# One transformer layer on one core: the first pair's operands used in place, the load of W_down moved, and three reorderings

## The reference

```
h      = rmsnorm(x) * (1 + scale1) + shift1
q,k,v,p = h @ w_in                       # 512 | 128 | 128 | 512 columns
merged = [rmsnorm(attention(q, k, v)), rmsnorm(causal_pool(p))]
x      = x + gate1 * (merged @ w_out)
h2     = rmsnorm(x) * (1 + scale2) + shift2
out    = x + gate2 * ((silu(h2 @ w_gate) * (h2 @ w_up)) @ w_down)   # 2816 wide
```

## Time and profile before

| | us |
|---|---|
| median of 3 runs (lowest, highest) | 1058.69 (1054.54, 1060.44) |
| the profiled execution | 1058.78 |
| its span, first to last instruction | 1057.0 |
| TensorE busy in it | 985.1 (93%) |
| VectorE busy | 701.2 (66%) |
| mean granted TensorE clock | 0.982 |

### The profile page before, as it was taken

One profiled execution on the slowest core, in us unless ns is written; L12 is line 12 of the kernel. 1 busy time (PEld: TensorE's weight loads), 2 busy tenths in 40 slices (PEclk: granted clock), 3 DMA queues, 4 the chain that ended last, 5 costly groups with the idle time before them and its releaser, 6 DMA issues.

```text
span 1057.0 us, 13418 instructions
## 1 busy us (share of the span) xinstructions
PE 985.1 (93%) x4656; PEld 822.1 (78%) x4656; DVE 701.2 (66%) x1089; ACT 379.3 (36%) x722; POOL 211.7 (20%) x167
## 2 busy tenths in 40 slices
PE   6979999989979849999999999999999999999998
PEld 6768888888867637878878787887878788787876
DVE  4658888784777857566566756656675666666554
ACT  2646667575333523123130412313041231304120
POOL 2033333334211005021110302111030211103010
PEclk9989999999999979999999999999999999999999
DMA  9935443255134196433344543334454343445223
GB/s 365 360 131 219 140 140 140 100 160 198 42 120 140 60 297 240 159 120 131 128 180 159 198 159 119 133 126 178 159 198 159 119 142 126 169 159 198 80 80 159
DMA packets 82725, 168.79 MB, mean 160 GB/s; under 512 B 5392, under 2 KB 50176, under 8 KB 82688
## 3 DMA queue, kind: packets, MB, share of 16 engines
q1 hardware_dynamic: 77456, 157.37, 41.9%
...
## 4 chain that ended last, share of the span: by engine, by line
PE 70%; DMA 10%; DVE 10%; ACT 3%; SPq 2%; issue 2%; POOL 1%; ACTq 0%; DVEq 0%
PE ps L1553 22%; PE ps L1555 21%; PE ps L1554 21%; DMA bs<-bs_scratch 7%; DMA wi_raw<-in_w_in 2%; PE ps L1664 1%; SPq L408 1%; DVE x L1179 1%; PE ps L1766 1%; SPq L410 1%; DMA bs_scratch<-stg 1%; DVE xn L1335 1%; DVE ring L1369 1%; DMA sinks<-in_attn_sinks 1%; DVE nmax L1248 1%
## 5 line engine op out<-in xcount | busy, mean ns | idle before, releaser
L1413 DVE TENSOR_TENSOR x<-x,ps 128x512 f32<-128x512 f32 x176 | 120.7, 686 | 83.6 <-PE ps L1555 82.8
L1025 POOL TENSOR_TENSOR wd_lo<-raw_d,wd_hi 128x1024 fp32r<-128x1024 f32 x22 | 57.4, 2627 | 425.7 <-ACT wd_hi L796 425.7
L1553 PE MATMUL ps<-h_hi,ring 128*128 128x512 f32 x352 | 138.1, 392 | 1.2 <-DVE h_lo L1362 0.9
L1554 PE MATMUL ps<-h_lo,ring 128*128 128x512 f32 x352 | 137.4, 390 | 0.0
L1555 PE MATMUL ps<-h_hi,ring 128*128 128x512 f32 x352 | 137.4, 390 | 0.0
L1553 PE MATMUL ps<-wd_hi,act_hi 128*128 128x512 f32 x352 | 136.9, 389 | 0.0
L1554 PE MATMUL ps<-wd_lo,act_hi 128*128 128x512 f32 x352 | 136.9, 389 | 0.0
L1555 PE MATMUL ps<-wd_hi,act_lo 128*128 128x512 f32 x352 | 136.9, 389 | 0.0
L1553 PE MATMUL ps<-bs,ring 128*128 128x512 f32 x264 | 106.0, 401 | 28.7 <-DMA bs<-bs_scratch 27.8
L1554 PE MATMUL ps<-bs,ring 128*128 128x512 f32 x264 | 104.5, 396 | 0.0
L1555 PE MATMUL ps<-bs,ring 128*128 128x512 f32 x264 | 104.2, 395 | 0.0
...
## 6 DMA issues: line engine op xcount, KB each, us to landing
...
raw_g<-in_w_gate SPq DMA_DIRECT2D x11, 1024.0 KB, 5.0
raw_u<-in_w_up SPq DMA_DIRECT2D x11, 1024.0 KB, 6.9
raw_d<-in_w_down SPq DMA_DIRECT2D x11, 1024.0 KB, 7.9
...
```

What stands on the lines that cost most here:

```text
L1025: pool.tensor_tensor(wd_lo[:, q, :], raw_d[:, q, :], wd_hi[:, q, :].bitcast(F32), ALU.subtract).then_inc(wd_lo_done, 1)
L1413: dve.tensor_tensor(xt, xt, bank(DB[j % 4]), ALU.add).then_inc(down_evac, 1)
L1553: pe.matmul(dst, s_hi, m_hi, start=start, stop=False, skip_group_check=onto)
L1554: pe.matmul(dst, s_hi, m_lo, start=False, stop=False, skip_group_check=onto)
```

## The change

1. `bs2`, two buffers of 8 KB per partition, takes T4. In the first pair T3 and T4 of tiles 6 and 7 are split straight into `bs` and `bs2`, at the columns where `S3` and `A22` read them. T3 and T4 of tiles 2 and 4 still go through the stage to DRAM and come back by three DMAs (`t_back`) after the last out-projection chain, whose buffers `bs` and `bs2` overlap. B22 goes through the stage for all four tiles. T3 and T4 of tiles 6 and 7 are also stored to DRAM, for the later pairs (`store_direct`).
2. In the order of tiles 2 and 4, B22 is split last.
3. `load_down` of pair p is issued behind the first stream of pair p; it was issued behind the last stream of pair p-1. That of pair 0 comes after the first pair's `A22`.
4. `m_low` of tiles 3 to 7 goes from GpSimd to VectorE, behind `mixed_sum(t, 1)`.
5. `bias_tiles` (VectorE) and the product on `wpl` (GpSimd) go behind the first tile's work of iteration 0; folds and scalings are spread anew.
6. ScalarE and VectorE: the rows of h2 ahead of the square; the first weight parts and sums ahead of `mixed_sum(6, 1)`; the fourth token sum a function of its own; tile 6's T3 ahead of `norm_x1(7)`.

```diff
+        bs2 = [place(f"bs2_{h}", [P, KT // 2, HALF], BASE + (104 + 16 * h) * KB, F32R) for h in range(2)]
...
-        FOLDS = (3, 5, 5, 5, 5, 1, 0, 0)
-        SCALED = ((), (), (), (), (), (0, 1, 2), (3, 4, 5), (6, 7))
+        FOLDS = (4, 4, 4, 4, 4, 4, 0, 0)
+        SCALED = ((), (), (), (), (), (), (0, 1, 2, 3, 4), (5, 6, 7))
...
-        T_ORDER = [(t, w) for t in (2, 4) for w in (T3, T4, B22, T2, T1)] + [
+        T_ORDER = [(t, w) for t in (2, 4) for w in (T3, T4, T2, T1, B22)] + [
...
-        STG_ORDER = [x for x in T_ORDER if x[1] in STREAMED]
+        STG_ORDER = [x for x in T_ORDER if x[1] == B22 or x[1] in STREAMED and x[0] < 6]
...
+            if (t, w) in STG_ORDER:
                 return stg[STG_ORDER.index((t, w)) % 2][:, low]
+            cols = slice(HALF1.index(t) * P, (HALF1.index(t) + 1) * P)
+            if w == T3:
+                return bs[:, :, low, cols]
+            if w == T4:
+                return bs2[low][:, :, cols]
...
-                    if not first and k < KT // 2 - 1:
-                        sp.wait_ge(bs_used, (KT // 2 - 1) * (3 * p + n - 1) + k + 1)
-                    elif not first:
+                    if k < KT // 2 - 1:
+                        sp.wait_ge(bs_used, (KT // 2 - 1) * (3 * p + n - 2) + k + 1)
+                    elif first:
+                        sp.wait_ge(prod_done, prod(0, S3, 1))
+                    else:
...
+            def store_direct(t, w):
+                sp.wait_ge(t_lo, T_ORDER.index((t, w)) + 1)
+                u = HALF1.index(t)
+                for h in range(2):
+                    sp.dma_start(bs_dram[STREAMED.index(w)][:, :, h, u * P:(u + 1) * P], t_dest(t, w, h).bitcast(F32)
+                                 ).then_inc(t_out, 16)
...
-            load_down(0, first=True)
-            store_stage(6, T3)
-            store_stage(7, T3)
-            store_stage(6, T4)
+            sp.wait_ge(stg_out[0], 32 * 3)
+            sp.wait_ge(stg_out[1], 32 * 3)
+            sp.dma_start(bs[:, :, :, 0:2 * P].bitcast(F32), bs_dram[0][:, :, :, 0:2 * P]).then_inc(t_back, 16)
+            for h in range(2):
+                sp.dma_start(bs2[h][:, :, 0:2 * P].bitcast(F32), bs_dram[1][:, :, h, 0:2 * P]).then_inc(t_back, 16)
+            store_direct(6, T3)
+            store_direct(7, T3)
+            store_direct(6, T4)
+            store_direct(7, T4)
+            load_raw(1, 0)
+            load_raw(1, 1)
+            store_stage(6, B22)
+            store_stage(7, B22)
+            sp.wait_ge(t_out, 32 * 4)
             sp.wait_ge(stg_out[0], 32 * 4)
             sp.wait_ge(stg_out[1], 32 * 4)
-            load_stream(0, 0, first=True)
-            store_stage(7, T4)
-            load_raw(1, 0)
-            load_raw(1, 1)
-            sp.wait_ge(stg_out[1], 32 * 5)
-            load_stream(0, 1)
-            store_stage(6, B22)
-            store_stage(7, B22)
-            sp.wait_ge(stg_out[0], 32 * 6)
-            sp.wait_ge(stg_out[1], 32 * 6)
-            load_stream(0, 2)
-            load_down(1)
+            load_stream(0, 2, first=True)
+            sp.wait_ge(prod_done, prod(0, A22, 1))
+            load_down(0, first=True)
             def pair_loads(p, last=False):
                 load_stream(p, 0)
+                load_down(p)
                 if not last:
                     load_raw(p + 1, 0)
                     load_raw(p + 1, 1)
                 load_stream(p, 1)
                 load_stream(p, 2)
-                if not last:
-                    load_down(p + 1)
...
+                if t - 1 in HALF1:
+                    h2_rows_act(t - 1)
                 square_x1(t)
                 if t - 1 in HALF0:
                     h2_high(t - 1)
-                if t - 1 in HALF1:
-                    h2_rows_act(t - 1)
...
-                if t == 6:
-                    act.wait_ge(g2_red_done, 1)
-                    a_high(0, A11, 0, 0, first=True)
-                    a_high(0, A11, 1, 0, first=True)
...
                     t_high(t - 1, T3)
                     t_high(t - 1, T4)
-                    t_high(t - 1, B22)
                     t_high(t - 1, T2)
                     t_high(t - 1, T1)
-            act.wait_ge(oa_chain, NT)
-            a_high(0, A12, 0, 0, first=True)
-            a_high(0, A12, 1, 0, first=True)
+                    t_high(t - 1, B22)
+                if t == 5:
+                    act.wait_ge(g2_red_done, 1)
+                    a_high(0, A11, 0, 0, first=True)
+                    a_high(0, A11, 1, 0, first=True)
+                    act.wait_ge(oa_chain, NT)
+                    a_high(0, A12, 0, 0, first=True)
+                    a_high(0, A12, 1, 0, first=True)
+            h2_rows_act(6)
             square_x1(7)
-            h2_rows_act(6)
+            act.wait_ge(t_back, 16 * 3)
+            t_high(6, T3)
             copy_p1(0, 0, first=True)
+            a_high(0, S2, 0, 0, first=True)
             norm_x1(7)
-            t_high(6, T3)
+            copy_p1(0, 1, first=True)
+            h2_rows_act(7)
             t_high(6, T2)
-            a_high(0, S2, 0, 0, first=True)
-            copy_p1(0, 1, first=True)
             a_high(0, S2, 1, 0, first=True)
-            h2_rows_act(7)
             t_high(7, T2)
             t_high(7, T3)
...
             act_high(silu_sb, 0, 0, 0, 1)
...
             second_half(0, 0)
+            down_high(0, first=True)
             with act.Fori(0, (NPAIR - 3) // 2) as j:
...
-
-            pool.wait_ge(const_in, 16 * 5)
-            pool.tensor_tensor(wpl[:, :, :], wpl[:, :, :], psc_bc, ALU.mult).then_inc(wpl_done, 1)
...
+                if it == 0:
+                    pool.wait_ge(const_in, 16 * 5)
+                    pool.tensor_tensor(wpl[:, :, :], wpl[:, :, :], psc_bc, ALU.mult).then_inc(wpl_done, 1)
...
-                if t + 3 < NT:
-                    m_low(t + 3)
...
-            bias_tiles()
...
+                if it == 0:
+                    bias_tiles()
...
-                dve.wait_ge(t_sum, n + 3)
+            def t_sum4(t):
+                xs = xn2[XBUF[PARTNER[t]]]
+                lo, up = slice(0, HALF), slice(HALF, D)
+                dve.wait_ge(t_sum, 4 * HALF1.index(t) + 3)
                 dve.tensor_tensor(xs[:, up], xs[:, up], xs[:, lo], ALU.subtract).then_inc(t_sum, 1)
...
             mixed_sum(0, 1)
             for t in range(1, NT):
                 if t + 1 < NT:
                     mixed_sum(t + 1, 0)
+                if t == NT - 2:
+                    a_low(0, A11, 0, 0)
+                    a_low(0, A11, 1, 0)
+                    dve.wait_ge(oa_chain, NT)
+                    a_low(0, A12, 0, 0)
+                    a_low(0, A12, 1, 0)
+                    a_sum13(0, 0, first=True)
+                    a_sum13(0, 1, first=True)
                 mixed_sum(t, 1)
+                if t + 2 < NT:
+                    m_low(t + 2)
                 if t < NT - 1:
                     h2_rows(t - 1)
+                    if t == NT - 2:
+                        a_sum2(0, 0, first=True)
                     if t - 1 in HALF0:
                         h2_low(t - 1)
                     else:
                         t_sums(t - 1)
+                        t_sum4(t - 1)
                         t_low(t - 1, T3)
                         t_low(t - 1, T4)
-                        t_low(t - 1, B22)
                         t_low(t - 1, T2)
                         t_low(t - 1, T1)
+                        t_low(t - 1, B22)
                     for k in FOLD2.get(t, ()):
                         fold_gate2(k)
-                if t == NT - 2:
-                    a_low(0, A11, 0, 0)
-                    a_low(0, A11, 1, 0)
-                    dve.wait_ge(oa_chain, NT)
-                    a_sum13(0, 0, first=True)
-                    a_sum13(0, 1, first=True)
-                    a_sum2(0, 0, first=True)
-                    a_sum2(0, 1, first=True)
-                    a_low(0, A12, 0, 0)
-                    a_low(0, A12, 1, 0)
+            a_sum2(0, 1, first=True)
             h2_rows(6)
             t_sums(6)
+            t_sum4(6)
             t_low(6, T3)
-            t_low(6, T2)
             a_low(0, S2, 0, 0)
-            a_low(0, S2, 1, 0)
             h2_rows(7)
             t_sums(7)
...
-            def stream_product(p, o, m, par, dst, start, n):
+            def stream_product(p, o, m, par, dst, start, n, direct=None):
                 pe.wait_ge(a_lo, prod(p, o, m))
-                if m == 0:
-                    pe.wait_ge(bs_in, 64 * (3 * p + n + 1))
+                if m == 0 and not direct:
+                    pe.wait_ge(bs_in, 64 * (3 * p + n - 1))
                 r = ring[m][(par + o) % 2]
                 for k in range(KT // 2):
-                    last = mm3(bank(dst[m]), r[:, 0, k, :], r[:, 1, k, :], bs[:, k, 0, :], bs[:, k, 1, :],
+                    b_hi, b_lo = (bs2[0][:, k, :], bs2[1][:, k, :]) if direct == T4 else (bs[:, k, 0, :], bs[:, k, 1, :])
```

(12 more changed lines are left out.)

17 lines of the change are left out of this document (12 added, 5 removed).

## The result

The changed kernel takes **1040.4 us** (median of 4 runs, 1040.1 to 1043.2) against 1059.0 us (4 runs of the kernel before beside it, 1054.5 to 1060.4). The ratio is 0.9837, its 95% interval 0.9803 to 0.9871: 1.3% to 2.0% faster. The span of the profiled execution went from 1057.0 to 1038.3 us. The forecast was 1040.4. The total is right; two of its terms are not, and they cancel.

What follows compares the result with a forecast made beforehand. TensorE was taken as the bound, busy 93% of the span, so only its waits and lower clock could yield time. Opening minus 4.8, x1 stage and first pair minus 13.6, W_down 0: 1058.8 - 18.4 = 1040.4 us, range 1033 to 1048.

Steps and rivals of the forecast that it cites:

- Opening, -4.8: Start of the kernel: TensorE's 5.7 us wait for `kn` goes, scores start at 67.6; minus 4.8 us, bounds 3 to 6.5.
- x1 stage: 260 to 350 us: five 1.7 us stalls, 4.9 us wait on `mixed_sum(6, 1)`, `A11` 3.2 us late; bounds minus 2 to plus 7.
- The price of the stretch: x1 stage: VectorE instructions meeting GpSimd's `m_low` ran longer (2.77 for 0.69 us); 2 us at five tiles.
- The sign that short waits leave the upper clock: x1 stage: after waits of 1.03 and 1.79 us the first product reads 0.47 and 0.50 us, taken as full clock.
- First pair: From 350 us: `S3` no longer waits for a stream, `S4` starts at 399 less 3.3 us.
- One sum without effect: First pair: W_down landed by 399, then scalings, copies and lows (5.2 + 2 + 5.2 us) end near 416, before `down(0)` at 425.
- W_down's load, 0 (bounds -2 to 0): Pair loop: issuing the load 11 us later changes nothing, since GpSimd's idle time covers it; 0 us, bounds minus 2 to 0.
- The argument from the last pair: Pair loop: the last pair loads no W_down yet waits 1.18 us, the same, so the load does not slow the stream.
- 1 (W_down held the stream up): Pair loop: W_down's load delayed the `S4` stream, so nine pairs' waits go (11.5 us): 1029 us; chance 0.12.
- 2: x1 stage and first pair: new waits eat most of the gain through lower clock and added work: 1051 us; chance 0.12.
- 3: First pair: the `S4` stream lands far too late, all lost after 411, 1063 us if at 415; chance 0.05.
- 4: First pair: it gives nothing because products wait for VectorE instead, only the opening is left: 1054 us; chance 0.05.

Runs made afterwards that it cites:

- e3: Kernel before, with only the bias tiles and GpSimd's product on `wpl` moved behind iteration 0's first work; 1053.3 us, ratio 0.9955.
- e9: Changed kernel with `m_low` of tiles 3 to 7 back on GpSimd, behind its rsqrt of the tile; 1038.9 us, ratio 0.9840.
- e2: Kernel before, with only W_down's load moved behind the first streamed load of its own pair; 1054.1 us, ratio 0.9965.
- e1: Changed kernel with W_down's load put back behind the third streamed load of the pair before; 1047.8 us, ratio 0.9904.
- e10: Kernel of e1, but from pair 1 on W_down's load brings 64 of 1024 columns (64 KB, not 1 MB); 1043.4 us, ratio 0.9879.
- e6: Changed kernel with pair 1's raw gate and up weights issued behind the stores of B22's last two tiles; 1044.8 us, ratio 0.9874.

## Why the prediction came out, step by step

- **Opening, -4.8**: right. -4.4 in the profiles, -4.8 alone (e3). The scores start at 66.99 us (67.6 forecast) behind 2.22 us of wait (3). The folds' new split cost nothing that shows: the out-projection starts at 254.88 us with it and at 255.30 in e3 without it.
- **x1 stage**: right in place and in size. Stalls of 1.64 us (1.7 forecast), four instead of five, the last one lying behind the products of `g2`. The wait on `mixed_sum(6, 1)` ended at 344.4 on the old clock (344.0) and was 4.66 us (4.9), with products of 0.63 us, the lower clock, until 344.2 (new clock) behind it. The price of the stretch, "2 us at five tiles", was right per meeting (2.1 us) and was met at four tiles in the kernel before (2.89, 6.19, 2.77 and 6.19 us for 0.75, 4.05, 0.69 and 4.05). What it was worth to TensorE was weighed too high: e9 brings all four back and is no slower. The sign that short waits leave the upper clock was read from the first product behind them (0.47 and 0.50 us), and that row cannot tell: behind 2.54 us of wait at 236.03 the kernel before reads 0.47 as well, and the granted clock in 236 to 246 us is 0.83. The conclusion was right by the clock itself, 1.00 in 295 to 300 and in 343 to 348 us.
- **First pair**: right in its chain, 3 to 4 us too optimistic. On the old clock: last transposes 363.3 (362.5), `S3` 377.8 (376.0), `S4` 399.8 (395.7). Three terms were too small. The three loads took 8.7 us from issue to ScalarE's start (347.41 to 356.12), not 7.5. The wait ahead of the transposes was 5.14 us, not about 4, and "the lower clock as before" lasted to 364.45, so `A12` ended 1.85 us late (372.35 for 370.5). And the stream: its first load went out at 387.3, 391.7 on the old clock, instead of 387.5. It waits until the stores of `B22` have landed, and these were issued at 383.0 to 387.4 on the old clock, where the prediction had the lows ready at 381.5 and all 3 MB out by 387.5. (Its own sum, 378.5 plus 3 MB at 390 GB/s, gives 386.6.) Its 8 us to landing were right. So this part and the x1 stage gave 10.0 us where 13.6 was written. One sum without effect is wrong as well: 399 plus 5.2 + 2 + 5.2 us is 411.4, not 416, for the end of W_down's lows. They ended at 415.8 on the old clock (411.44), since the load landed later, and `down(0)` waited for nothing.
- **W_down's load, 0 (bounds -2 to 0)**: this step failed. It is worth 3.7 us in the kernel before (e2; 2.4 in its profile) and 7 in the changed one (e1). The argument from the last pair, whose wait of 1.18 us was "the same" without a W_down load, used one value of a quantity that scatters: the last pairs of the old place read 1.18, 1.70 and 1.08 us, the whole effect is 0.27 us per pair, and nine times that is 2.4 us. One row could not have excluded it. Nor is the last pair a control: over ten profiles of the new place its wait is 1.40 us on average where the eight pairs ahead of it have 1.04, and in the old place 1.32 where they have 1.36. It loads no raw weights either and so differs in more than W_down; what sets its wait stays open. In the two profiles at hand the term looked like 4.3 us, of which nearly half is scatter. The second part is an interaction: I priced the load's new place with GpSimd's idle time alone, and did not ask what the old place would cost once the first pair ended earlier and `load_down(0)` stood behind its `A22`. It would have been 4.7 us (e1), 3.3 of them gone with the bytes (e10). The page DMA: Bandwidth & Descriptors of the Trainium skill, section "Queues, rings and completion order", states that each DMA engine consumes descriptors in ring order, and also that a later one may finish its write before an earlier one. So its rule gave no ground for a term of zero. No row here shows single descriptors, but e10 shows that what is issued behind the loads of a stream can matter to it: 10.6 us for 12.5 with 64 KB in place of 1 MB.
- **Rivals.** 1 (W_down held the stream up) was true in kind and far too large: it took the whole 11.5 us of the waits for the load's, and 9.7 of 12.2 remain whatever its place. 2 took the new waits as dear as the old ones; the four short stalls brought no lower clock (granted 1.00 in 270 to 300 us), as forecast. 3 and 4 did not occur; only in e6 did `S4` wait for VectorE, which itself waited for the raw weights. The prices of 3 were wrong: a stream that lands at 415 instead of 395.7 adds 19.3 us to 1040.4, which is 1059.7 and not 1063, and from 414 on the kernel is as slow as before, not slower.

The sum, 18.4, is thus 4.8 + 13.6 + 0 forecast against 4.4 + 10.0 + 4.3 in the profiles: two errors near 4 us of opposite sign. That the total agrees to 0.1 us is luck, and so is part of the third term, of which near 2 us are scatter. With either error alone the time would have missed the forecast by about 4 us and still lain inside its range of 1033 to 1048. What was right is the place of each stall and, in the opening and the x1 stage, its size.
